# A decoder step's second mixer: from one stretch behind its input projection to small blocks between the projection's tiles

## The reference

```
z = x @ w_in                              # u (1024), v (1024), o_pre (1024), gates (8)
uc = conv_b + sum_j full[:, j:j+L] * cw[j]   # causal, width 4, over u
q, k = split(silu(uc))
# per head, with b = cumsum(log_sigmoid(fg)), ic = ig
m_t = max(max_s(b_t - b_s + ic_s), b_t + m);  d = exp(log_d - m_t);  w_prev = exp(b + m - m_t)
scores = (q @ k.T) * d
h = (scores @ v + w_prev * (q @ C)) / max(|sum(scores) + w_prev * (q . n)|, exp(-m_t))
C_new = w_c * C + sum_s w_s k_s v_s^T;  n_new = w_c * n + sum_s w_s k_s
h = (h - mean(h)) * rsqrt(var(h) + EPS) * hn_w
out = (sigmoid(o_pre) * h) @ w_out;  x = layernorm(ALPHA * x + out)
```

## Time and profile before

| | |
|---|---|
| median of 3 runs (lowest, highest) | 1705.7 us (1701.45, 1709.63) |
| profiled execution | 1704.81 us, its span 1702.0 us |
| mean granted clock of TensorE | 0.948 |
| busy share: PE, DVE, ACT, POOL | 92%, 75%, 64%, 3% |
| experts (from about 685 us) | some 60% of the span |

### The profile page before, as it was taken

One profiled execution on the slowest core, in us unless ns is written; L12 is line 12 of the kernel. 1 busy time (PEld: TensorE's weight loads), 2 busy tenths in 40 slices (PEclk: granted clock), 3 DMA queues, 4 the chain that ended last, 5 costly groups with the idle time before them and its releaser, 6 DMA issues.

```text
span 1702.0 us, 24481 instructions
## 1 busy us (share of the span) xinstructions
PE 1570.5 (92%) x8634; PEld 1360.4 (80%) x8634; DVE 1281.5 (75%) x1557; ACT 1097.7 (64%) x1352; POOL 53.9 (3%) x45
## 2 busy tenths in 40 slices
PE   7999799896996875999999999999999999999995
PEld 6888799894995665787887887887887887888884
DVE  4635466654746344799999998999999998999994
ACT  5445544344532333787887877877887877877884
POOL 0000000000003310000000000000000000000000
PEclk9999899998986687899999999999999999999998
DMA  8432545564530041699899899899999998998990
GB/s 329 144 116 100 173 174 178 195 226 189 165 115 29 0 186 67 249 372 381 332 366 372 346 367 357 343 370 354 355 383 341 365 378 322 370 379 341 376 368 35
DMA packets 53281, 451.31 MB, mean 265 GB/s; under 512 B 6713, under 2 KB 6913, under 8 KB 20961
## 3 DMA queue, kind: packets, MB, share of 16 engines
q1 hardware_dynamic: 47808, 423.74, 65.2%
q0 software_dynamic: 2864, 16.85, 2.8%
q10 hardware_dynamic: 2544, 9.86, 1.5%
HBM read 439.84 MB, written 10.59 MB: 265 GB/s over the span
## 4 chain that ended last, share of the span: by engine, by line
PE 90%; DVE 4%; ACT 4%; issue 1%; DMA 1%; DVEq 0%; ACTq 0%; SPq 0%; POOL 0%; POOLq 0%
PE bank L542 26%; PE bank L543 26%; PE bank L544 26%; PE bank L537 2%; PE bank L981 1%; PE bank L827 1%; PE bank L782 1%; PE bank L787 1%; ACT X L1259 1%; PE bank L645 1%; ACT whi L1405 1%; DMA ring<-in_w_in 0%; PE bank L1013 0%; PE bank L1014 0%; PE bank L883 0%
## 5 line engine op out<-in xcount | busy, mean ns | idle before, releaser
L1929 DVE TENSOR_TENSOR wlo<-ring,whi 128x1024 fp32r<-128x1024 f32 x672 | 806.2, 1223 | 72.8 <-ACT whi L1405 31.7
L1405 ACT ACTIVATE whi<-ring 128x1024 fp32r<-128x1024 f32 x672 | 711.0, 1065 | 196.5 <-PE bank L544 194.7
L542 PE MATMUL bank<-whi,high 128*128 128x512 f32 x1344 | 532.5, 396 | 16.5 <-DVE low L2046 15.1
L544 PE MATMUL bank<-whi,low 128*128 128x512 f32 x1344 | 526.5, 392 | 0.0
L543 PE MATMUL bank<-wlo,high 128*128 128x512 f32 x1344 | 525.7, 391 | 0.0
L542 PE MATMUL bank<-high,whi 128*128 128x264 f32 x1008 | 295.9, 294 | 38.4 <-DVE wlo L1479 12.5
L542 PEld LDWEIGHTS bank<-whi,high 128*128 128x128 f32 x1344 | 254.1, 189 | 70.5 <-DVE wlo L1929 17.0
L544 PEld LDWEIGHTS bank<-whi,low 128*128 128x128 f32 x1344 | 253.5, 189 | 53.5
L543 PEld LDWEIGHTS bank<-wlo,high 128*128 128x128 f32 x1344 | 254.3, 189 | 51.2
L543 PE MATMUL bank<-low,whi 128*128 128x264 f32 x1008 | 292.3, 290 | 0.0
L544 PE MATMUL bank<-high,wlo 128*128 128x264 f32 x1008 | 291.9, 290 | 0.0
(11 more groups left out here) (320 smaller groups left out, 1111.6 us busy)
## 6 DMA issues: line engine op xcount, KB each, us to landing
ring<-in_w_moe SPq DMA_DIRECT2D x224, 1536.0 KB, 8.6
ring<-in_w SPq DMA_DIRECT2D x22, 1024.0 KB, 4.7
ring<-in_w_in SPq DMA_DIRECT2D x14, 1024.0 KB, 5.3
ring<-in_w_in SPq DMA_DIRECT2D x8, 1536.0 KB, 7.1
ring<-in_w SPq DMA_DIRECT2D x7, 1536.0 KB, 6.7
ring<-in_w_out SPq DMA_DIRECT2D x4, 1536.0 KB, 6.3
state<-in_state ACTq DMA_DIRECT2D x1, 4096.0 KB, 12.4
o_Cs<-state POOLq DMA_DIRECT2D x1, 4096.0 KB, 13.0
```

Source lines behind the costliest of these rows:

```text
L542: pe.matmul(out, xh, wh, start=start, stop=False)
L544: return pe.matmul(out, xl, wh, start=False, stop=stop)
L1405: A_(whi[:, g % NSPLIT, :], ring[:, s % RING, (g % 3) * D:(g % 3 + 1) * D], ACT.Copy).then_inc(whi_ready, 1)
L1929: V.tensor_tensor(wlo[:, g % NSPLIT, :], ring[:, s % RING, (g % 3) * D:(g % 3 + 1) * D], whi[:, g % NSPLIT, :].bitcast(F32), ALU.subtract) ...
```

## The change

The second mixer is cut into small blocks. `IN1_LOADS` loads the tiles of `w_in1` in pairs and single tiles, in an order that brings q, k and v of a head early; `behind1` says which results come behind which tile, and the three engines' programs are written out in that order. The list of parts:

- PE: the gate logits stand behind two tiles, in two column groups of one pass over the input; the state products have 32 columns of queries as weights, a pair of samples' states as input (512 columns), and one column group per head; the result is turned, and DVE picks the diagonal. Sample values are no longer spread by PE.
- ACT: the first tap of the convolution, Silu and Sigmoid from Exp and Ln, the absolute value of a sum; each layer norm loads the table set with Ln and Exp in one.
- DVE: the other taps straight from the bank; everything else in pieces between the tiles' low parts.
- Sample values: ACT takes the rows, GpSimd stores them, and broadcasts each sample's row of 1024 values from memory to 128 partitions. ACT scales it by the keys, and DVE adds it to the decayed state, in the loop of the residual.

```diff
+IN1_LOADS = [(0, 4), (8, 9), (1, 5), (2, 3), (10, 11), (6,), (12, 13), (7,), (14, 15), (16, 17), (18, 19), (20, 21), (22, 23)]
+IN1 = [i for l in IN1_LOADS for i in l]
+QK1 = [i for i in IN1 if i < 2 * MH]
...
-        jobs += ["gi", "gf"] + [("y", i) for i in range(20)]
-        for g in range(PAIRS):
-            jobs += [("y", 20 + g), ("ns", g)]
...
+        behind1 = {1: ["gg"], 3: [("vt1", 0)], 5: ["acol", "fw", ("bc", 0), ("bc", 1)], 6: [("kt1", 0), ("sc1", 0)],
+                   7: [("kt1", 1), ("sc1", 1)], 8: [("en", 0), ("num", 0), ("den", 0)], 9: [("C", 0), ("vt1", 1)],
+                   10: [("ns", 0), ("en", 1)], 11: [("num", 1), ("den", 1)], 12: [("ns", 1), ("hm", 0)],
+                   13: [("C", 1), ("tns", 0), ("bc", 2)], 14: [("kt1", 2), ("sc1", 2), ("ns", 2)],
+                   15: [("vt1", 2), ("tns", 1), ("hm", 1)], 16: [("en", 2), ("num", 2), ("den", 2)],
+                   17: [("bc", 3), ("kt1", 3), ("sc1", 3), ("ns", 3)],
+                   18: [("vt1", 3), ("tns", 2), ("tns", 3), "qn", ("vs1", 0), ("vs1", 1)],
+                   19: [("en", 3), ("num", 3), ("den", 3)], 20: [("hm", 2), ("hv", 0)], 21: ["hms", ("hm", 3), ("C", 2)],
+                   22: [("hv", 1), ("hv", 2), "hvs"], 23: [("hv", 3), ("C", 3)]}
+        for s in range(24):
+            jobs += [("y", IN1[s])] + behind1.get(s, [])
...
+            def gate_logits():
+                pe.wait_ge(x_ready, 2 * KD)
+                out = job("gg")
+                for c in range(KD):
+                    for i in range(2):
+                        mm = pe.matmul(out[32 * i:32 * i + MH, 0:N], wgate[:, c, i * MH:(i + 1) * MH], X[:, c, :],
+                                       start=(c == 0), stop=(c == KD - 1))
...
+            def state_products(p):
+                out = job(("ns", p))
+                for h in range(MH):
+                    mm = pe.matmul(out[32 * h:32 * h + 32, :], qk[:, h, N - 32:N], Cs[:, h, 2 * p:2 * p + 2, :], start=True, stop=True)
...
-            def spread_two(h):
-                for b in SAMPLES_BEHIND[h]:
-                    pe.wait_ge(vs1_ready, 2)
-                    for i in range(2):
-                        spread(job(("wb", b, i)), b, lambda v: v[:, i * 512:(i + 1) * 512])
...
+            T = TIN1
+            projection(T, T + 2, 3)
+            gate_logits()
+            projection(T + 2, T + 4, 3)
+            value_turns(0)
+            projection(T + 4, T + 6, 3)
+            row_columns()
+            spread_row("bc", 0)
+            spread_row("bc", 1)
+            projection(T + 6, T + 7, 3)
+            key_scores(0)
+            projection(T + 7, T + 8, 3)
+            key_scores(1)
+            projection(T + 8, T + 9, 3)
+            weighted_values(0)
+            projection(T + 9, T + 10, 3)
+            final_state(0)
+            value_turns(1)
+            projection(T + 10, T + 11, 3)
+            pe.wait_ge(state1_loaded, 16)
+            pe.wait_ge(qk_ready, max(QK1.index(h) for h in range(MH)) + 1)
...
+            projection(T + 19, T + 20, 3)
+            weighted_values(3)
+            projection(T + 20, T + 21, 3)
+            head_mean(2)
+            head_square(0)
+            projection(T + 21, T + 22, 3)
             pe.wait_ge(hs_ready, 1)
-            for h in range(MH):
-                done(product(job(("hm", h))[:, 0:N], lambda c: ones, lambda c: h1[:, 2 * h + c, :], 2))
-            for h in range(MH):
-                pe.wait_ge(hsq_ready, h + 1)
-                done(product(job(("hv", h))[:, 0:N], lambda c: ones, lambda c: hsq[:, 2 * h + c, :], 2))
-            pe.wait_ge(y1_ready, MH)
+            done(product(job("hms")[:, 0:MH * NS], lambda c: ones, lambda c: h1[:, c:KD:2, NP_:N], 2))
+            head_mean(3)
+            final_state(2)
+            projection(T + 22, T + 23, 3)
+            head_square(1)
+            head_square(2)
+            pe.wait_ge(hssq_ready, 1)
+            done(product(job("hvs")[:, 0:MH * NS], lambda c: ones, lambda c: hssq[:, c:KD:2, :], 2))
+            projection(T + 23, T + 24, 3)
+            head_square(3)
+            final_state(3)
...
-                A_(spare, one, ACT.Ln)
+                if n != 2:
+                    nc.scalar.preload_act_table_set("natural_log_exp_and_others")
...
+            def tap(i):
+                n = QK1.index(i)
+                z = see(act, ("y", i))
+                if n >= 3:
+                    act.wait_ge(qk_ready, n - 2)
+                A_(uc[:, n % 3, :], z[:, 0:N], ACT.Identity, scale=vec_("convw3", i), bias=vec_("convb", i)).then_inc(tap_ready, 1)
+                A_(tail[:, i, :], z[:, NP_ - 3:NP_], ACT.Copy).then_inc(tap_ready, 1)
+                A_(us[:, i, 3, :], z[:, NP_:N], ACT.Copy).then_inc(tap_ready, 1)
...
+                own.settle(A_(sg[:, n % 2, :], uc[:, n % 3, :], ACT.Exp, scale=-1.0))
+                own.settle(A_(sg[:, n % 2, :], sg[:, n % 2, :], ACT.Ln, bias=one))
+                A_(sg[:, n % 2, :], sg[:, n % 2, :], ACT.Exp, scale=-1.0).then_inc(sg_ready, 1)
...
+            take_final_state(3)
+            for i in range(NSPLIT):
+                round_tile(TOUT1 + NSPLIT + i)
+                for b in (2 * i, 2 * i + 1):
+                    act.wait_ge(vb1_loaded[b], 16)
+                    for h in range(MH):
+                        own.start(A_(vb1[b][:, h * MDV:(h + 1) * MDV], vb1[b][:, h * MDV:(h + 1) * MDV], ACT.Copy,
+                                     scale=ki[:, h, b:b + 1]))
+                    own.wait()
...
+                    if n == 2 and k < KD - 1:
+                        new_sample_state(k)
+                        if k == 0:
+                            new_sample_state(KD - 1)
...
+            def convolution(i):
+                n = QK1.index(i)
+                u, s = see(dve, ("y", i)), uc[:, n % 3, :]
+                dve.wait_ge(tap_ready, 3 * n + 3)
+                for d in range(1, 4):
+                    w = vec_(f"convw{3 - d}", i)
+                    own.start(V.scalar_tensor_tensor(out=s[:, d:NP_], in0=u[:, 0:NP_ - d], scalar=w, in1=s[:, d:NP_],
+                                                     op0=ALU.mult, op1=ALU.add))
+                    own.start(V.scalar_tensor_tensor(out=s[:, NP_:N], in0=us[:, i, 3 - d, :], scalar=w, in1=s[:, NP_:N],
+                                                     op0=ALU.mult, op1=ALU.add))
+                    own.wait()
+                dve.nop().then_inc(freed(("y", i)), 1)
...
+                dve.wait_ge(dabs_ready, h + 1)
+                own.settle(V.tensor_tensor(t, t, see(dve, ("en", h))[:, 0:NP_], ALU.max))
+                own.settle(V.reciprocal(t2, t))
+                own.settle(V.tensor_tensor(h1[:, 2 * h:2 * h + 2, 0:NP_],
+                                           see(dve, ("num", h))[:, :].rearrange("p (v n) -> p v n", v=2),
+                                           bc(t2.unsqueeze(1), [P, 2, NP_]), ALU.mult))
...
+            def new_sample_state(b):
+                dve.wait_ge(kv_ready, b + 1)
+                for h in range(MH):
+                    own.start(V.scalar_tensor_tensor(out=Cs[:, h, b, :], in0=Cs[:, h, b, :], scalar=fwb[:, h, 1, b:b + 1],
+                                                     in1=vb1[b][:, h * MDV:(h + 1) * MDV], op0=ALU.mult, op1=ALU.add))
...
-                Pv.tensor_tensor(Cs[:, h], Cs[:, h], bc(fwb[:, h, 1, :].unsqueeze(2), [P, NS, MDV]), ALU.mult)\
-                    .then_inc(pool_own, 1)
-                n += 1
-            pool.wait_ge(pool_own, n)
+                if h == 2:
+                    pool.wait_ge(vrow1_ready, 1)
+                    pool.dma_start(vrows, vrow1).then_inc(vrow1_stored, 16)
+                    pool.wait_ge(vrow1_stored, 16)
+                pool.wait_ge(cout_ready, h + 1)
+                pool.dma_start(A["o_Cp"][:, h], Cout[:, h % 2, :]).then_inc(stored1, 16)
+            pool.wait_ge(qn_ready, 1)
+            pool.dma_start(A["o_ns"], n0).then_inc(stored1, 16)
+            pool.wait_ge(psum_ready, J[("C", MH - 1)] + 1)
             for b in range(NS):
-                pool.wait_ge(kv_ready, b + 1)
-                Pv.tensor_tensor(Cs[:, :, b, :], Cs[:, :, b, :], kvb[b % 2], ALU.add).then_inc(cnew_ready, 1)
-            pool.wait_ge(cout_ready, MH)
-            pool.dma_start(A["o_Cp"], Cout).then_inc(stored1, 16)
-            pool.dma_start(A["o_ns"], n0).then_inc(stored1, 16)
+                if b == 4:
+                    pool.wait_ge(xl_ready, 5 * KD)
+                pool.dma_start(vb1[b], bc(vrows[b:b + 1], [P, D])).then_inc(vb1_loaded[b], 16)
```

751 lines of the change are left out of this document (445 added, 306 removed).

## The result

| | time, us | against the kernel before |
|---|---|---|
| before | 1703.58 (median of 4, 1700.51 to 1709.63) | |
| after | 1642.43 (median of 4, 1640.84 to 1646.32) | 0.9642, 95% interval 0.962 to 0.9664 |

The change takes off 61.1 us; forecast were 1639.5 us and a range of 1623 to 1660. The profiled execution of after took 1646.32 us, the slowest of its four, so 58.5 us less than the profiled one of before.

The account below looks back on a forecast made before the run. It took no engine as full in layer 1's mixer: they wait in turn, TensorE partly at low clock. Centring 580.3 against 643.9 gives -63.6, later layer norms -2.6: 1704.8 - 66.2 = 1638.6, median 1639.5 us, range 1623 to 1660.

Parts of the forecast that it names:

- T: Layer 1's input projection: the last tile ends at 529.8 us, instead of about 514, with blocks between the tiles.
- Column groups that overlap: Blocks between the tiles: state products of a pair take 1.06 us in four column groups, gate logits 3.5 in two.
- one late slot at the second head's scores: Behind projection tile 7, the second head's scores wait 3 us for a convolution and a product queued on VectorE.
- the stall behind sample 7: Output projection: sample 7 waits for all 32 scalings, holding low halves of output tiles 5 to 7; TensorE idles some 9 us.
- everything starts 2.6 us earlier: Start of the rebuilt piece: two of four layer-norm table loads, 1.28 us each, stand ahead of it and leave the path.
- the two later layer norms, -2.6: Sum: the two later layer norms lose their table loads, taking another 2.6 us off after the centring's -63.6.
- The 0.39 us of the first pass behind column groups: Next tile's first pass lasts 0.39 us against 0.28 elsewhere; ten column-group changes cost about 1 us, 0.1 each.
- the 13 us that the change gives back: Output projection's end: the centring comes 40 us after its start instead of 28.6, giving back some 13 us.
- The queues held the tiles: Rival: ScalarE's and VectorE's fixed orders cost each tile about a microsecond, 15 us more, 1655 us; chance 0.15.
- The clock did not stay low: Rival: the clock stays low from first to last projection tile, 5.3 us per tile, +54, 1694 us; chance 0.02.
- The broadcasts did not land one after another: Rival: the eight sample-value broadcasts land singly, 15.4 us each, the end 97 us later, 1736 us; chance 0.02.
- the end does not stall: Rival: VectorE's 24 us at the end run beside the eight output tiles, to T+37.5, 1626.5 us; chance 0.10.

Follow-up runs that it names:

- e1: The changed kernel with sample 7's state made after the last residual instead of after the first; 1633.08 us, ratio to before 0.9583.
- e5: The changed kernel without ScalarE's scaling of sample values and without the new sample states on VectorE; 1626.43 us, ratio to before 0.9542.
- e10: The changed kernel, scalings spread, VectorE's states 0-4 after residuals 0-4, 5-6 between layer norm 2's centring and scaling, 7 behind it; 1624.39 us, 0.9542 of before.
- e2: The changed kernel, scalings spread, VectorE's states 0-3 after residuals 3-6, 4-7 between layer norm 2's centring and scaling; 1627.26 us, ratio to before 0.9544.
- e4: The changed kernel with the one-column state products of before instead of the 512-column products in column groups; 1652.56 us, ratio to before 0.9715.
- e12: The changed kernel's work, all blocks but gate logits behind the last projection tile, in before's order, head after head; 1659.20 us, ratio to before 0.9745.
- e6: The changed kernel with all blocks but the gate logits behind the last projection tile, in its own order among themselves; 1651.76 us, ratio to before 0.9694.
- e3: The kernel before with only the layer norms' edit, one table set with Ln and Exp loaded ahead; 1698.49 us, ratio to before 0.9972.
- e8: The kernel before with its one-column state products replaced by the change's 512-column products in column groups; 1688.61 us, ratio to before 0.9918.
- e9: The kernel before without any sample state update (spread products, ScalarE's scaled copies, GpSimd's work); 1676.31 us, ratio to before 0.9852.
- e11: The kernel before with the table-load edit, column-group state products and no sample state update together; 1659.50 us, ratio to before 0.9747.

## Why the prediction was right, and what its terms were off by

| step | forecast | after's trace |
|---|---|---|
| last low half of the layer norm's output begins | 416.45 - 2.6 = 413.85 | 415.99 |
| gate logits begin, behind two tiles | 414.7 + 1.6 + 3.05 = 419.4 | 420.96 |
| gate logits; state products of a pair | 3.5; 1.06 | 3.73; 1.06 |
| TensorE's waits between the tiles | 5 (3 of it at one place) | 5.24 (3.37 at that place) |
| last projection tile's end, T | 529.8 | 532.80 (the last square starts) |
| first output tile | T+10.4 | T+11.5 (544.30) |
| ScalarE's last scaling | T+29.7 | T+31.6 (560.90 + 3.53) |
| wait before output tile 5 | some 9 | 11.33 |
| centring | 580.3 | 585.35 |
| from the centring to the router | 11.61 - 1.28 = 10.33 | 598.74 - 585.35 = 13.39 |

**Right for its reasons.** Column groups that overlap, full clock in the blocks, one late slot at the second head's scores, and the stall behind sample 7: each is in the trace at its place, and e1 shows the last one to be the cause (9.3 us by an edit of one line's place). VectorE from sample 7 to the centring took 20.84 us for a forecast of 20.8; that it fits so closely is in part luck, since the seven states came out 0.9 us shorter in all than the sum has them, and the residuals and handovers longer by about as much. The landing of the broadcasts was covered but for 1.28 us.

**Off in size.** The terms miss 8.1 us in the profiled execution: 5.05 at the centring and 3.06 in layer norm 2.

The largest part of the first, 2.1 us, is the step *everything starts 2.6 us earlier*: the last low half came at 415.99, only 0.5 us before that of the kernel before. The table loads are gone; but in after's execution TensorE's mean clock from 40 to 135 us, in layer 0, was 0.96 and in before's 1.00, and the first layer norm's centring came 1.9 us later (179.29 for 177.41). The instructions up to there are the same. e5's execution has 1.00, and its last low half came at 413.61, as forecast; its row of this stretch:

```profile
40.00:135.00 95.00, 92.88 (x745) 83.56 (x745) 46.19 (x76) 44.89 (x81) 1.13 (x2) 1.00 0.40 136
```

Another 0.9 us came up to T, the first output tile cost 1.1 more, and ScalarE 0.8. There the first scaling waited 1.28 us for its broadcast: GpSimd issued the first one at 542.01, T+9.2 and not T+2, since its queue first waited for ScalarE's copy of the last state; scalings of 0.44 us for 0.47 took part of that back. T itself scatters, from 530.45 (e5) to 535.88 (e1), by the start and by the tile behind the wait of 3.37 us, which ran at full clock in after, e5 and e10 and not in e1, e2 and e4, 2.4 us apart.

The 3.06 us are the step *the two later layer norms, -2.6*: the load is gone, but TensorE, which the states had kept waiting for residuals, ran the variance products at the lower clock, 6.82 us for 3.80 [the row at 586.73]. e10 and e5, without those waits, have 3.80 us and 10.3 us from centring to router, as forecast.

The medians differ from the forecast by only 2.9 us, and that is partly luck: the profiled execution, for which 1638.6 us were forecast, took 7.7 us more, but it was also 3.9 us above the median of its four, and the forecast of the median had 0.9 us added.

Two readings were off without moving the sum. The 0.39 us of the first pass behind column groups were put down to the change of groups; but behind products without column groups, too, the first pass of a tile takes 0.37 in before (at 87.68 us), so the change itself takes some 0.02 us. And the 13 us that the change gives back around the states set before's time from the start of the output projection beside after's from the end of its first tile. From the first pass to the centring it is 28.6 us in before, 47.7 in after (537.64 to 585.35) and 31.0 in e10 (537.25 to 568.26): 19 us given back, of which e10 gets 17 again.

**What the prediction left unsaid.** It read the earlier trace rows as engines that wait in turn, and one could take from it that the gain comes from filling these waits. By the medians, 1703 becomes 1659 with after's work in before's order (e12), 1652 with the heads interleaved among themselves (e6) and 1642 with the tiles between them: 44, 7 and 9 us. In the 44 the state update, put back at the end, already counts against it with some 16 (what e5 shows for after). On the other side e3, e8 and e9 name 41 to 46 us (table loads, one-column products, state update). The rest, some 16 us, no run isolates. Its places, by the traces: the gate logits, 8.82 us in e11 and 3.73 in e12; from the last quotient to the output projection, 20.8 us in e11 (551.57 to 572.35) and 12.6 in e12 (541.10 to 553.67); the heads, 10.0 us apart in e11 and 9.2 in e12. The wait and the products of the gate logits in e11:

```profile
415.98 8.82 PE L535 MATMUL bank<-X,wgate 128*4 128x264 f32 x32 [8.02 <-ACT X L1253]
```

**The rivals.** The queues held the tiles for no more than the 5 us taken. The clock did not stay low between the tiles. The broadcasts did not land one after another: eight of 512 KB landed in a median of 7.4 us. That the end does not stall came true only by e1, e2 and e10.

## What to carry to other kernels

Before blocks are woven between tiles, run them in one stretch in their new form: here that kept 52 of 61 us, 44 even in the old order, and showed that most of the gain was work taken away or made lighter, and not the weaving. Look at an engine's queue for an instruction that waits for the last of a series: put ahead of pieces that another engine soon needs, it cost 9 us here; moved to places where nobody waits, all eight states cost nothing that the times show (e10 beside e5). Work that has been moved off one stretch is not gone until the stretch where it arrives has been read slot by slot, the clock of the engine that it keeps waiting included.
